# Linear attention of a decoder layer: the second head pair's levels between the last projections

## The reference

```python
def gla_chunked(q, k, v, log_a):
    # S_t = diag(a_t) S_(t-1) + k_t^T v_t ;  o_t = q_t S_t  (inclusive of t)
    ...
    def step(state, inp):
        q_c, k_c, v_c, g_c = inp
        b = jnp.cumsum(g_c, axis=2)
        o_inter = jnp.einsum('bhtk,bhkv->bhtv', q_c * jnp.exp(b), state)
        diff = b[:, :, :, None, :] - b[:, :, None, :, :]
        decay = jnp.where(causal[:, :, None], jnp.exp(jnp.minimum(diff, 0.0)), 0.0)
        scores = jnp.einsum('bhtk,bhsk,bhtsk->bhts', q_c, k_c, decay)
        o_intra = jnp.einsum('bhts,bhsv->bhtv', scores, v_c)
        ...
    ...
    o_gla = rmsnorm(o_gla.transpose(0, 2, 1, 3), gla_norm_g.reshape(GLA_HEADS, GLA_DV))
    o_gla = o_gla.reshape(B, S, GLA_VW) * jax.nn.silu(g_r)
```

## Time and profile before

| | us |
|---|---|
| median of 3 runs (1310.09 to 1311.79) | 1310.1 |
| the profiled execution | 1311.84 |
| its span, first to last instruction | 1310.2 |
| TensorE busy | 1210.2 |
| VectorE busy | 901.6 |
| ScalarE busy | 740.0 |
| GpSimd busy | 305.8 |

### The profile page before, as it was taken

One profiled execution on the slowest core, in us unless ns is written; L12 is line 12 of the kernel. 1 busy time (PEld: TensorE's weight loads), 2 busy tenths in 40 slices (PEclk: granted clock), 3 DMA queues, 4 the chain that ended last, 5 costly groups with the idle time before them and its releaser, 6 DMA issues. The chain is left out here.

```text
span 1310.2 us, 18132 instructions
## 1 busy us (share of the span) xinstructions
PE 1210.2 (92%) x6596; PEld 916.1 (70%) x6596; DVE 901.6 (69%) x844; ACT 740.0 (56%) x760; POOL 305.8 (23%) x273
## 2 busy tenths in 40 slices
PE   3999999999999979899828999999999999999975
PEld 3777787876888768588715777777777777777742
DVE  3365757474574267344667988989998998998825
ACT  5365646463532333412146777787777778777613
POOL 1000000001111011100150444444444444444400
PEclk8999999999999995899959999999999999999988
DMA  5210101001110020453239999999999999999747
GB/s 176 65 33 17 33 17 33 17 17 37 45 34 17 1 97 33 163 182 109 85 118 390 396 396 386 382 383 381 383 389 387 382 381 385 384 384 393 299 167 316
DMA packets 83152, 271.63 MB, mean 207 GB/s; under 512 B 14640, under 2 KB 45472, under 8 KB 58528
## 3 DMA queue, kind: packets, MB, share of 16 engines
q1 hardware_dynamic: 72640, 248.31, 50.8%
q0 software_dynamic: 9312, 18.45, 4.3%
q10 hardware_dynamic: 1152, 4.19, 0.8%
HBM read 253.91 MB, written 25.79 MB: 213 GB/s over the span
## 5 line engine op out<-in xcount | busy, mean ns | idle before, releaser
L1984 PE MATMUL ps<-w_high,in_hi 128*96 128x512 f32 x512 | 204.0, 398 | 4.9 <-DVE hid L1912 2.9
L1984 PE MATMUL ps<-w_lower,in_hi 128*96 128x512 f32 x512 | 202.1, 395 | 0.0
L1984 PE MATMUL ps<-w_high,in_lo 128*96 128x512 f32 x512 | 201.6, 394 | 0.0
L1254 POOL DMA_INDIRECT x_g<-h_dram,who x33 | 155.6, 4714 | 40.8 <-POOL who L1250 27.8
L1926 DVE TENSOR_TENSOR d_lo<-cat,d_hi 128x2048 fp32r<-128x2048 f32 x64 | 146.2, 2286 | 24.6 <-ACT d_hi L1848 24.6
L1898 DVE TENSOR_TENSOR w_lower<-w_raw,w_high 128x2048 fp32r<-128x2048 f32 x62 | 141.7, 2285 | 24.6 <-ACT w_high L1827 24.6
L1903 DVE TENSOR_TENSOR w_lower<-w_raw,w_high 128x2048 fp32r<-128x2048 f32 x64 | 143.4, 2279 | 4.3 <-PEq L1333 4.3
L1833 ACT ACTIVATE w_high<-w_raw 128x2048 fp32r<-128x2048 f32 x62 | 118.9, 1919 | 24.2 <-PE ps L1984 24.2
L1848 ACT ACTIVATE d_hi<-cat 128x2048 fp32r<-128x2048 f32 x64 | 122.2, 1911 | 17.2 <-PEq L1333 13.8
L1827 ACT ACTIVATE w_high<-w_raw 128x2048 fp32r<-128x2048 f32 x62 | 118.3, 1908 | 0.6 <-DMA w_raw<-exp_w_gate 0.5
L510 DVE TENSOR_TENSOR_SCAN prod<-cat 128x256 f32<-128x256 f32 (+7 forms) x64 | 83.4, 1345 | 41.7 <-ACT cat L438 41.6
(11 more groups left out here) (293 smaller groups left out, 2413.4 us busy)
## 6 DMA issues: line engine op xcount, KB each, us to landing
w_raw<-exp_w_gate SPq DMA_DIRECT2D x64, 1024.0 KB, 10.4
w_raw<-exp_w_up SPq DMA_DIRECT2D x64, 1024.0 KB, 11.8
cat<-exp_w_down SPq DMA_DIRECT2D x64, 1024.0 KB, 11.1
w_raw<-w_in SPq DMA_DIRECT2D x22, 512.0 KB, 3.8
xt<-x SPq DMA_DIRECT2D x8, 512.0 KB, 7.5
w_raw<-w_out SPq DMA_DIRECT2D x8, 512.0 KB, 4.8
x_g<-x SPq DMA_DIRECT2D x8, 512.0 KB, 3.8
x_dram<-cat SPq DMA_DIRECT2D x8, 512.0 KB, 4.9
```

The source lines that it names most:

```text
L1254: pool.indirect_dma_start(x_g[0:CAP, j, :], None, k["h2_dram"][:, :], bass.IndirectOffsetOnAxis(ap=who[j][0:CAP, 0:1], axis=0), bounds_che ...
L1984: mm = pe.matmul(out, x_[:, n // 3, :], w_[:, n // 3, :], start=(n == 0), stop=(n == 3 * KD - 1))
```

## The change

The two head pairs' fourteen levels (`g` = 0 to 13) form one pipeline on all engines. The second pair's v is projected before its gate (`TILE_COLS`), so the halves 12 to 15 are now v and 16 to 19 the gate. TensorE does level 6 right behind level 5, half 13, and the first pair's outputs, and the halves 14 to 19 lie between the sums, the second pair's levels 7 to 12, its turns, own terms and updates. Levels 12 and 13 and the second outputs stand behind the last half. `outputs` first does the sixteen v matmuls of a pair and then the fourteen of the state, and signals once at its end. The second pair's turn of v goes through banks 2 and 3 twice, its own terms go head by head (`diagonal_of`, `own_terms`), and its gate is evicted raw into `cat` and its sigmoid taken at the end (`sigmoids_1`, `gate_1`). The first pair's squares and norm factors lie in other buffers (`norm_place`), the second pair's decay factors in `vT`. `sums` waits for both gated products. The loads of w_out start after the last low half instead of after the last projection.

```diff
-        return 4 + n % 4 if n < 4 else 4 + n % 2 if n < 8 else n % 2 if n < 16 else 6 + n % 2
+        return 4 + n % 4 if n < 4 else 4 + n % 2 if n < 8 or n in (14, 15) else n % 2
+
+    def turn_bank(p, n):
+
+        return (2 if p else 6) + n
...
     def sum_banks(p, h):
-        return ps[:, 4 + 2 * h * p:6 + 2 * h * p, :]
+        return ps[:, 4 * p + 2 * h:4 * p + 2 * h + 2, :]
+
+    def norm_place(p, h):
+        return kl[:, h] if p else b_all[:, 0] if h else low
...
                 sp.wait_ge(lo_done, t - 2)
                 sp.dma_start(w_raw[:, t % 3], w_dram[:, :, TILE_COLS[t]:TILE_COLS[t] + P]).then_inc(w_in_s[t % 3], 16)
-            sp.wait_ge(projd, 2 * LAST)
+            sp.wait_ge(lo_done, LAST)
             for kd in range(KD):
+                if kd == 3:
+                    sp.wait_ge(cat_done, 2)
+                if kd == 4:
+                    sp.wait_ge(ql_done, LEVELS)
+                    sp.wait_ge(kl_done, LEVELS)
+                    sp.wait_ge(own_done, 4)
+                    sp.wait_ge(dec, 2)
                 if kd == 6:
-                    sp.wait_ge(ql_done, GLA_PAIRS * LEVELS)
-                    sp.wait_ge(kl_done, GLA_PAIRS * LEVELS)
+                    sp.wait_ge(ql_done, STEPS)
+                    sp.wait_ge(kl_done, STEPS)
+                    sp.wait_ge(own_done, 8)
+                    sp.wait_ge(dec, 4)
                 sp.dma_start(wo_raw[kd], a["w_out"][0, kd * P:(kd + 1) * P, :]).then_inc(wo_in[kd], 16)
...
+            for kd in range(2):
+                split_wo(kd)
+            place_level(12)
+            place_level(13)
+            for kd in range(2, SB_PAIRS):
                 split_wo(kd)
             dve.wait_ge(cathi, 1)
             dve.tensor_tensor(w_lo[:, 0, 0:SB_PAIRS], cat[:, 0:SB_PAIRS, 0:P], w_hi[:, 0, 0:SB_PAIRS].bitcast(F32),
                               ALU.subtract).then_inc(catlo, 1)
+            gate_1(0)
+            gate_1(1)
             gate_out(1)
-            split_wo(KD - 1)
+            for kd in range(SB_PAIRS, KD):
+                split_wo(kd)
             normed(1)
...
@@ -1084,7 +1157,11 @@
                 elif n in (6, 7):
                     pe.wait_ge(r_done, n - 5)
                 elif n in (8, 9):
-                    pe.wait_ge(pred_done, 4)
+                    pe.wait_ge(own_done, n - 6)
+                elif n in (14, 15):
+                    pe.wait_ge(pred_done, 14)
+                elif n in (16, 17):
+                    pe.wait_ge(ln_done, 2)
                 elif n >= 8:
                     pe.wait_ge(out_done, n - 1)
...
             def turn_v(p):
-                pe.wait_ge(out_done, 4 if p == 0 else HALVES)
-                if p == 0:
+                pe.wait_ge(out_done, 16 if p else 4)
+                if p:
+                    pe.wait_ge(ln_done, 3)
+                else:
                     pe.wait_ge(x_done, 4)
-                else:
-                    pe.wait_ge(cat_done, 2)
                 for n in range(4):
+                    if p and n >= 2:
+                        pe.wait_ge(v_done, 4 * p + n - 1)
                     for m in range(4):
                         t, h = 2 * n + m // 2, m % 2
-                        mm = pe.transpose(ps[:, n, m * P:(m + 1) * P], vT[:, h, t * P:(t + 1) * P], ident[:])
+                        src = gate_place(1, h) if p else vT[:, h]
+                        mm = pe.transpose(ps[:, 2 + n % 2 if p else n, m * P:(m + 1) * P], src[:, t * P:(t + 1) * P],
+                                          ident[:])
                     mm.then_inc(vturn, 1)
...
             def outputs(p):
-                pe.wait_ge(pred_done, PREDS * (p + 1))
-                if p == 0:
-                    pe.wait_ge(out_done, 16)
+                pe.wait_ge(pred_done, 2 * LEVELS * (p + 1))
+                pe.wait_ge(own_done, 4 * (p + 1))
+                pe.wait_ge(state_done, (NT - 1) * (p + 1))
                 pe.wait_ge(dec, 2 * p + 2)
-                for t in range(NT):
+                for h in (1, 0):
+                    if h == 0:
+                        pe.wait_ge(out_done, 20 if p else 14)
+                    for t in range(NT):
+                        pe.matmul(ps[:, 2 * h + t // 4, (t % 4) * P:(t % 4 + 1) * P], v[:, t, h * DV:(h + 1) * DV],
+                                  s_all[:, h, t, :], start=(t % 4 == 0), stop=False)
+                for t in range(1, NT):
                     for h in range(2):
-                        pe.matmul(ps[:, 2 * h + t // 4, (t % 4) * P:(t % 4 + 1) * P], v[:, t, h * DV:(h + 1) * DV],
-                                  s_all[:, h, t, :], start=True, stop=(t == 0))
-                    for h in range(2 if t else 0):
                         rows = slice(DK * h, DK * (h + 1))
                         mm = pe.matmul(ps[:, 2 * h + t // 4, (t % 4) * P:(t % 4 + 1) * P], k_dec[rows, t - 1, :],
-                                       vT[rows, 0, t * P:(t + 1) * P], start=False, stop=True)
-                    if t:
-                        mm.then_inc(o_ready, 2 if t == 1 else 1)
+                                       vT[rows, 0, t * P:(t + 1) * P], start=False, stop=(t % 4 == 3))
+                mm.then_inc(o_ready, 1)
 
             def sums(p, h):
-                pe.wait_ge(sq_done, 2 + 2 * p + h + 1)
-                if h and not p:
-                    pe.wait_ge(ln_done, 2)
+                pe.wait_ge(gated, 2 * p + 2)
+                pe.wait_ge(sq_done, 2 * p + h + 1)
+                src = e[:, h] if p else norm_place(0, h)
                 for hf in range(2):
-                    mm = pe.matmul(sum_banks(p, h)[:, hf, :], ones[:], e[:, h, hf * HALF:(hf + 1) * HALF], start=True, stop=True)
+                    mm = pe.matmul(sum_banks(p, h)[:, hf, :], ones[:], src[:, hf * HALF:(hf + 1) * HALF], start=True, stop=True)
                 mm.then_inc(summed, 1)
...
-            level(0, 0)
-            for l in range(1, LEVELS):
-                project(8 + l - 1)
-                level(0, l)
+            level(0)
+            for g in range(1, 6):
+                project(7 + g)
+                level(g)
+            level(6)
+            project(13)
+            outputs(0)
             project(14)
+            for h in range(2):
+                sums(0, h)
             project(15)
-            outputs(0)
+            level(7)
+            turn_v(1)
             project(16)
-            sums(0, 0)
+            level(8)
+            diagonal_of(1, 0)
             project(17)
-            sums(0, 1)
+            level(9)
+            diagonal_of(1, 1)
             project(18)
+            turn_k(1)
+            level(10)
+            updates(1)
+            level(11)
             project(19)
-            turn_v(1)
-            diagonal(1)
-            turn_k(1)
-            updates(1)
-            for l in range(LEVELS):
-                level(1, l)
+            level(12)
+            level(13)
             outputs(1)
             for h in range(2):
                 sums(1, h)
-            pe.wait_ge(gated, 4)
-            pe.wait_ge(sq_done, 6)
             pe.wait_ge(catlo, 1)
             pe.wait_ge(wolo, SB_PAIRS)
```

More of the change, by code:

```diff
@@ L1000, in split_wo @@
                 dve.tensor_tensor(wo_lo[kd], wo_raw[kd], wo_hi[kd].bitcast(F32), ALU.subtract).then_inc(wolo, 1)
-            def levels(p):
-                place_level(p, 0)
-                for l in range(3, LEVELS + 2):
-                    if l < LEVELS:
-                        exponents(p, l)
-                    if l <= LEVELS:
-                        queries(p, l - 1)
-                    place_level(p, l - 2)
-                    if p == 0 and l in (3, 5, 7):
-                        split_lo(first + 6 + l // 2 - 1)
             for n in range(4):
@@ L1038, in _ @@
             take_k(0)
-            diagonal(0)
+            own_terms(0, 0)
+            own_terms(0, 1)
             split_lo(first + 4)
-            queries(0, 0)
+            queries(0)
             gate_0(6)
-            exponents(0, 2)
+            exponents(2)
             gate_0(7)
             states(0)
-            queries(0, 1)
+            queries(1)
             split_lo(first + 5)
-            levels(0)
-            split_lo(first + 9)
-            gates_1()
-            dve.wait_ge(r_done, 6)
-            gate_out(0)
-            normed(0)
-            dve.wait_ge(cat_done, 2)
-            to_tile_end(1)
-            take_v(1)
-            decayed(1)
-            exponents(1, 0)
-            exponents(1, 1)
+            place_level(0)
+            exponents(3)
+            queries(2)
+            place_level(1)
+            split_lo(first + 6)
+            exponents(4)
+            queries(3)
+            place_level(2)
+            exponents(5)
+            queries(4)
+            place_level(3)
+            split_lo(first + 7)
+            exponents(6)
+            queries(5)
+            place_level(4)
+            exponents(7)
+            queries(6)
+            place_level(5)
+            exponents(8)
```

(38 more changed lines are left out.)

297 lines of the change are left out of this document (170 added, 127 removed).

## The result

The changed kernel takes 1290.4 us (median of four runs, 1290.2 to 1292.0). The kernel before took 1310.1 beside it. The ratio is 0.985, with a 95% interval of 0.984 to 0.987. So 19.7 us are gained, where 15.1 were forecast. The time lies inside the range (1286.8 to 1299.5), between the forecast and rival (a). The profiled execution took 1290.5 us, with a span of 1288.9.

A forecast was written before the change was run, and what follows sets the result against it. TensorE bounds the kernel, losing idle time and half clock in the second pair's work. Second outputs 16.3 us earlier, less 1.4 before the sums, is 14.9, put at 15.1 for a later clock fall: 1310.1 - 15.1 = 1295.0, range 1286.8 to 1299.5.

The forecast's parts named there:

- rival (a): Second outputs and sums: the clock holds to the stage's end, gain 21.9 us, 1288.2 in total; chance 18%.
- 2.6, 2.8 and 2.6: Forecast TensorE idle times in us: at the second turn of v, before the second outputs, and before the second sums.
- Gap one: Second pair's turn of v: TensorE waits 2.6 us for VectorE to place level 7 and copy v back.
- rival (c): Inside the pipeline, VectorE is late, costing 1 to 2 us at each of three places: about 1299; chance 11%.
- Outputs of the first pair: TensorE's queue before the second outputs: taken at 7.9 us as before, 1 us either way for both passes.
- The sum of 8.2: Outputs in two passes: cost of 30 matmuls from v and state group times, 8.2 us, beside 7.9 unchanged.
- own terms: Second pair's own terms in TensorE's queue before the second outputs: taken at 2.0 us.
- the first pair's sums: Two sums steps in TensorE's queue before the second outputs: 1.88 us per head, taken at 3.8.
- once at half, the outputs did not bring it back: Second outputs: after the clock falls they stay at 0.50, taking 14.1 us as before instead of 7.9.
- Rival (b): Second turn of v: the clock falls there too, losing 1.7 to about 2.2 us, 1297 in total; chance 17%.
- (d): Between 454 and 491 us: the clock stays down until the sums, roughly +33, net 1328, slower than before; chance 4%.
- The forecast's shift of its sum onto the median: Whole kernel: gain of 15.1 taken from the median 1310.1, giving 1295.0, not from the profiled 1311.8, giving 1296.7.

The follow-up runs named there:

- e5: Changed kernel with the two low halves of w_out moved behind placing levels 12 and 13 on VectorE: 1292.8 us, 0.982 of the kernel before.
- e6: Changed kernel with the second pair's v copied ahead of placing level 7 on VectorE: 1289.6 us, 0.980 of the kernel before.
- e7: Changed kernel with each of the second pair's sums waiting only for its own square: 1290.9 us, 0.981 of the kernel before.
- e4: Changed kernel with the state pass of both pairs' outputs head by head instead of alternating heads: 1297.4 us, 0.988 of the kernel before.
- e2: Changed kernel with only the second pair's outputs by turns of v and state matmuls again: 1300.7 us, 0.990 of the kernel before.
- e3: Kernel before with both pairs' outputs in two passes, order otherwise as before: 1307.3 us, 0.994 of the kernel before.
- e8: Changed kernel with v copied before placing level 7, w_out low halves behind levels 12 and 13, sums awaiting own squares: 1288.3, again 1283.2 us; both 0.979 of before.
- e9: Same three moves as e8, plus one more high half of w_out put behind the second pair's squares on ScalarE: 1282.0 us, 0.978 of the kernel before.

## Why the prediction came out as it did

**Right, and for the reasons given.** The place and the size of the idle time: gaps of 2.5 (the turns of v took 4.17 with it and 1.67 without; the row shows 2.07 of it as idle time), 2.96 and 2.65 against 2.6, 2.8 and 2.6, each ended by the instruction that was named. (Gap one was added up a little high: 3.1 less 0.8 is 2.3, not 2.4.) e5, e6 and e7 confirmed their contents by taking them out. VectorE kept up at levels 8 to 11 (rival (c) false: no wait there), the w_out loads cost nothing, and the stages behind stayed at 772. The second outputs began at 494.46, against 495.9.

**That start hides errors of opposite sign.** Outputs of the first pair were taken at 7.9, plus or minus 1; they took 5.5. The sum of 8.2 that was set beside the 7.9 does not come out: 32 v instructions at 1.06 for 8 are 4.2, 28 state instructions at 0.42 for 4 are 2.9, together 7.2. The rows thus did point to a gain, though a smaller one, for these are pieces of the form by turns, each with its changes between full-row and half-row matmuls. And the own terms were taken at 2.0 as before. They took two rows of 1.9, 3.9 in all (458.57 and 468.01), because the change does one head behind level 8 and the other behind level 9. The x32 row at 362.07, with both heads by turns, has the same sixteen matmuls in 2.06. It is what e4 showed for the state pass. The third is the first pair's sums, taken at 3.8: that is twice the 1.88 of a row whose end is modelled; from their start to the next matmul the two heads took 3.03 (436.00 to 439.03). What is left, 0.3 us early, is spread over the levels and turns; the seven half projections took 39.7, as forecast.

**The step that failed is "once at half, the outputs did not bring it back".** The fall came where it was forecast, behind two levels and 2.96 us idle (0.72 in the gap, 0.50 from 494.5). The rule of the Trainium skill that was named above ("TensorE: Matmul & The Clock Gate", section "HAM oscillation — how this bites in real kernels"), which puts the fall at longer gaps, is against the trace here too: 2.96 us were enough. But the row the step rested on, 14.1 us at 0.50, shows the outputs by turns, and e2 and e3 show that the form decides. In all eleven profiles with two passes the state pass stood at full clock (1.83, or 3.05 in e4); nine of them had begun the outputs at half. Both kernels with turns in the second outputs stayed at half for 14.1 us. So the forecast took 14.1 for a term that measured 8.1. This also spoils a sign that the forecast gave: outputs of 8 us were to mean rival (a), a clock that holds, but here 8.1 us hold some 5 at half clock. The sums, taken at 4.55 from their start to the next matmul, took 4.83 here, and 3.14 in e7 and in the changed kernel's second profile, as the next fall happens to land. The 3.8 that was set for them at full clock is again twice the modelled 1.88.

Summed up on the stage: forecast 14.9; outputs of the first pair +2.4, own terms -1.9, the first pair's sums +0.8, other pieces +0.3, second outputs +6.0, sums to norm and the difference in gaps -0.4: 22.1, as measured. Rival (a) gave 21.9 with the clock holding; the size agrees by chance, its mechanism was not there in this run. Rival (b) was, in the runs of e4 and e5. Of (d) there is no sign: nowhere between 453 and 487 does the clock stay down.

**Of the total**, 19.7 us of medians stand against 21.3 in the two spans. The kernel before varies by 4 us between its runs (1307.8 to 1311.8), its profiled execution was at the upper end, and stages outside took 0.7 more. The forecast's shift of its sum onto the median was needed and right in kind.

**Open:** what in the v pass brings the clock back, and why it takes from 3.0 to 6.1 us of it. By the rows of the changed kernel and e2 TensorE is busy throughout in both forms; the weight loads are busy 5.00 of 5.00 us in the v pass and 10.87 of 14.10 by turns. No run here separates that from the kind of matmul.

## What to carry to other kernels

When the diff changes in what order the same matmuls are issued, price it as a new operation: half-row matmuls of two heads side by side cost 1.8 us for fourteen, 3.05 head by head, and mixed with full-row ones the whole block costs 7.9 instead of 5.5. A clock reading belongs to the form of work on which it was taken; before carrying "it stays at half" over, ask whether the work there is still the same. And after one gap is closed read again which engine ends the next: the sums waited for VectorE, then for ScalarE, and in e8 their gap was 2.96 us in one profile and 1.55 in the other.

## What was not expected of the hardware

- Neighbouring matmuls on different halves of the rows overlap: 28 instructions in 1.83 us by turns of head, 3.05 head by head; own terms 2.06 against 3.9.
- At half clock, 23 us of levels with 21.1 busy and 14.1 us of outputs by turns left it at 0.50; sixteen full-row matmuls in a row had it back at 1.00 each time, in nine profiles, 3.0 to 6.1 us after their start (510.3 to some 514.6 in e3, 494.5 to some 499.7 after; the shortest is the second run of e8, the longest e4).
- A gap of 1.44 us behind two levels was enough for a fall in e5 and in the second run of e8, not in the first, nor in e9; 2.96 was in all seven profiles that have it. The 2.06 us at the second turn of v had a fall in two profiles of seven (e4 and e5).
